# Twelve first units of weights loaded one stage ahead, two loading stages folded away, and sixteen places for the gathers of a mixture of experts

## The reference, cut to what matters

```python
def reference(x, ...):
    x = first_block(x, ...)    # x + [sparse attention | gated MLP] @ w_out, then x + conv feed-forward (width 2816)
    x = second_block(x, ...)   # four mixers, each w_branch product gated by sigmoid(x @ w_gate + b), w_out, layer norm;
                               # then x + sigmoid(x @ w_ple_gate + b) * (p @ w_ple), layer norm
    return third_block(x, ...) # modulated norm of x and of a context of 256 tokens, projections, two attentions, w_out,
                               # then a mixture of experts, and a last rms norm

def moe(h, ...):               # 32 experts, the 4 best of each token
    top_v, top_i = lax.top_k(h @ router_w + router_b, 4)
    ...                        # rows sorted by expert in blocks of 128, each block through its expert
    contrib = ys[dest] * gate_sorted[:, None]
    return jax.ops.segment_sum(contrib, tok_sorted, num_segments=T)
```

## Time and profile before

| | |
|---|---|
| median of 3 runs | 4125.99 us (4120.43 to 4131.15) |
| the profiled execution | 4129.73 us, its span 4127.9 us |
| PE busy | 3511.0 us (85%) |
| DVE busy | 2328.0 us (56%) |
| ACT busy | 1536.9 us (37%) |
| POOL busy | 140.4 us (3%) |
| mean granted clock of PE | 0.913 of 2.4 GHz |
| DMA | 653.53 MB, 158 GB/s over the span |
| experts' stage | from about 2820 us to 4061 us |

### The profile page before, as it was taken

How to read it: one execution, slowest core, us unless ns; L and a number is a source line. 1 busy time by engine, 2 the same in 40 slices (tenths; PEclk the granted TensorE clock), 3 DMA queues, 4 the chain that set the end, 5 groups by cost and what they waited for, 6 DMA issues and landing times. The chain is left out here.

```text
span 4127.9 us, 45959 instructions
## 1 busy us (share of the span) xinstructions
PE 3511.0 (85%) x15671; PEld 2637.0 (64%) x15672; DVE 2328.0 (56%) x2916; ACT 1536.9 (37%) x1926; POOL 140.4 (3%) x124
## 2 busy tenths in 40 slices
PE   6778798999958688899879778775999999999996
PEld 4646687774446457688652645554777777777774
DVE  3355675338232245445440547435888888888885
ACT  1143332010023431110110215314777777777772
POOL 0000000000000100000000000002000000000001
PEclk8889999999979899699989889977999999999997
DMA  4311222222111100022216300116999999999995
GB/s 144 104 47 42 82 91 93 77 95 82 62 36 46 32 11 1 27 95 99 81 61 232 102 31 19 34 58 273 387 361 366 353 362 365 355 350 363 363 351 197
DMA packets 172315, 653.53 MB, mean 158 GB/s; under 512 B 14953, under 2 KB 82377, under 8 KB 114226
## 3 DMA queue, kind: packets, MB, share of 16 engines
q1 hardware_dynamic: 154370, 605.44, 40.2%
q0 software_dynamic: 7568, 25.70, 1.7%
q10 hardware_dynamic: 10272, 20.98, 1.3%
HBM read 610.98 MB, written 36.77 MB: 157 GB/s over the span
## 5 line engine op out<-in xcount | busy, mean ns | idle before, releaser
L378 DVE TENSOR_TENSOR experts_rest<-experts_weights,experts_leading 128x2048 fp32r<-128x2048 f32 x384 | 875.3, 2286 | 100.1 <-ACT experts_leading L2894 100.1
L2894 ACT CAST experts_leading<-experts_weights 128x2048 fp32r<-128x2048 f32 x384 | 715.4, 1904 | 46.9 <-ACT experts_y L2886 23.1
L384 PE MATMUL psum<-experts_leading,experts_xT_leading 128*128 128x512 f32 x1024 | 409.3, 400 | 51.6 <-DVE experts_rest L378 51.6
L385 PE MATMUL psum<-experts_rest,experts_xT_leading 128*128 128x512 f32 x1024 | 406.8, 397 | 0.0
L386 PE MATMUL psum<-experts_leading,experts_xT_rest 128*128 128x512 f32 x1024 | 402.5, 393 | 0.0
L384 PEld LDWEIGHTS psum<-experts_leading,experts_xT_leading 128*128 128x128 f32 x1024 | 194.6, 190 | 107.8 <-DVE experts_rest L378 65.4
L386 PEld LDWEIGHTS psum<-experts_leading,experts_xT_rest 128*128 128x128 f32 x1024 | 194.4, 190 | 44.6
L385 PEld LDWEIGHTS psum<-experts_rest,experts_xT_leading 128*128 128x128 f32 x1024 | 194.9, 190 | 40.2
L384 PE MATMUL psum<-experts_leading,experts_hidden_leading 128*128 128x512 f32 x512 | 210.3, 411 | 0.0
L386 PE MATMUL psum<-experts_leading,experts_hidden_rest 128*128 128x512 f32 x512 | 202.0, 394 | 0.0
L385 PE MATMUL psum<-experts_rest,experts_hidden_leading 128*128 128x512 f32 x512 | 200.9, 392 | 0.0
(11 more groups left out here) (664 smaller groups left out, 6923.2 us busy)
## 6 DMA issues: line engine op xcount, KB each, us to landing
experts_weights<-in_w_up SPq DMA_DIRECT2D x256, 1024.0 KB, 6.9
experts_weights<-in_w_down SPq DMA_DIRECT2D x128, 1024.0 KB, 6.8
merge_weights<-in_w_merge SPq DMA_DIRECT2D x32, 768.0 KB, 4.2
ada_weights<-in_w_ada SPq DMA_DIRECT2D x24, 1024.0 KB, 6.8
ff_up_weights<-in_w_up SPq DMA_DIRECT2D x22, 1024.0 KB, 4.8
expert_rows<-experts_y ACTq DMA_DIRECT2D x66, 256.0 KB, 7.2
down_weights<-in_w_down SPq DMA_DIRECT2D x16, 704.0 KB, 5.1
out_weights<-in_w_out SPq DMA_DIRECT2D x6, 1536.0 KB, 8.7
```

The source lines that it names most:

```text
L378: return dve.tensor_tensor(out, src, leading.bitcast(F32), ALU.subtract)
L384: pe.matmul(out, lh, rh, start=start, stop=False)
L385: pe.matmul(out, lh, rl, start=False, stop=False)
L2894: act.copy(leading[h % LEADING], place(ring, h)).then_inc(masked, 1)
```

## The change

`FirstUnit` sets a place for one unit of weights at the top of SBUF (`Core.high`), with semaphores of its own (242 to 247), and `load` issues its DMAs in whatever stage calls it. The stage that uses the unit takes that place as place 0 of its ring and skips the load of unit 0. By the code there are twelve such units: proj1, out1, the up stage, proj2a, proj2b, proj2c, merge, out2, ple, proj3, proj3b and out3. Their loads are issued on SP in the stage ahead: in a norm (proj1, ff_up, proj2c, merge, proj3, proj3b), at the start of an attention (out1, out3), in the short `glu` stage (proj2b), or at the end of SP's list in down1 (proj2a), merge (out2) and out2 (ple).

In the opening of these stages DVE now splits the first cut (or unit) first and then all source chunks; PE waits chunk by chunk. In `feed_forward_up`, `gated_products` (first branch) these waits stand inside the loop body and are passed for every unit.

The per-layer input is loaded in out2, and the stage `ple_in` is gone with its barrier; the context is loaded in the layer norm at the end of the second block (`ln2`), and `ctx_in` is gone; the zeros are cleared by POOL in `rope_diff`. In `combine` there are sixteen places, no gather waits for a sum, and the residual's load waits for the seventh gather.

```diff
+EARLY = (242, 244, 246)
...
+    def high(self, name, shape, below=0):
+        at = self.nc.sbuf_top // 32 * 32 - below - 4 * math.prod(shape[1:])
+        assert self.nc.sbuf_base <= at, name
+        t = self.nc.alloc_sbuf_tensor_at(name, shape, F32, offset=at)
...
         with nc.Block() as block:
-            if memory:
+            if memory or then:
                 @block.sync
                 def _(sp):
+                    if then:
+                        then(sp, sem)
...
+class FirstUnit:
+    def __init__(self, k, name, pieces, size, below=0):
+        self.slot = k.high(f"{name}_first", [P, size], below)
+        self.at = k.places[-1]
+        first = EARLY[k.early % len(EARLY)]
+        k.early += 1
+        self.pieces = pieces(self.slot)
+        self.landed = [k.nc.alloc_semaphore(f"{name}_first{c}_landed", num=first + c) for c in range(len(self.pieces))]
+
+    def load(self, sp, sem):
+        for (place, src), landed in zip(self.pieces, self.landed):
+            sp.dma_start(place, src).then_inc(landed, 16)
+
+    def retire(self, k):
+        k.retired += self.landed
+        k.places.remove(self.at)
+
+def first_unit(k, name, section, below=0, size=None):
+    unit = section.weights[0, :, :]
+    return FirstUnit(k, name, lambda slot: [(section.cut(slot, c), section.cut(unit, c)) for c in range(len(section.cuts))],
+                     size or section.kc * section.columns, below)
...
-def project(k, name, sections, beside=None, room={}):
+def project(k, name, sections, beside=None, room={}, first=None, then=None):
...
-        ring = sb("weights", [P, 2, size])
-        landed = [[sem(f"weights{i}_half{c}_landed") for c in range(2)] for i in range(2)]
+        ring = [first.slot if first and i == 0 else sb(f"weights{i}", [P, size]) for i in range(2)]
+        landed = [first.landed if first and i == 0 else [sem(f"weights{i}_half{c}_landed") for c in range(2)] for i in range(2)]
...
+                        if first and q == 0 and isinstance(u, int) and u == 0:
+                            return
                         sp.wait_ge(emptied[slot], turn * s.chunks + done0[q][slot])
...
-                                half = s.kc // 2 or s.kc
-                                if j == 0 and s.split and source_chunks and kk in (0, half):
-                                    pe.wait_ge(source_split, source_chunks - s.kc + (s.kc if kk else half))
+                                opens = isinstance(u, int) and u == 0
+                                if j == 0 and s.split and source_chunks and (kk == 0 or opens):
+                                    pe.wait_ge(source_split, source_chunks - s.kc + (kk + 1 if opens else s.kc))
...
+                if first:
+                    split_unit(0, 0, starts[0] % 2, 0, only=0)
                 split_source(range(own // 2))
-                split_unit(0, 0, starts[0] % 2, 0, only=0)
+                if not first:
+                    split_unit(0, 0, starts[0] % 2, 0, only=0)
                 split_source(range(own // 2, own))
...
 def feed_forward_up(k, src, out, first):
...
-                            if j == 0 and kk in (0, KD // 2):
-                                pe.wait_ge(source_split, KD if kk else KD // 2)
+                            if j == 0:
+                                pe.wait_ge(source_split, kk + 1)
...
+                split_unit(0, 0)
                 for kk in range(KD):
-                    if kk == KD // 2:
-                        split_unit(0, 0)
                     dve.wait_ge(source_masked, kk + 1)
...
 def gated_products(..., first, then=None):
...
-                            if q == 0 and (j, kk) in ((0, 0), (0, kc_gate // 2), (1, 0)):
-                                pe.wait_ge(source_split, (kc_gate // 2 if kk == 0 else kc_gate) if j == 0 else kc_gate + kc)
+                            if q == 0 and (j == 0 or kk == 0):
+                                pe.wait_ge(source_split, kk + 1 if j == 0 else kc_gate + kc)
...
-                split_source(source_gate, gate_parts, kc_gate // 2, 0)
                 split_unit(0, 0)
-                split_source(source_gate, gate_parts, kc_gate, 0, lo=kc_gate // 2)
+                split_source(source_gate, gate_parts, kc_gate, 0)
                 split_source(source(0), parts[0], kc, kc_gate)
...
-    with k.stage("ple_in", within=True) as (sb, sem):
-        per_layer = sb("p", [P, PLE // P, T])
...
+    def ple_loads(sp, sem):
         landed = sem("p_landed")
+        sp.dma_start(per_layer[:, :, :], k.dram["pT"].rearrange("(c p) t -> p c t", p=P)).then_inc(landed, 16)
+        w_ple.load(sp, sem)
+        sp.wait_ge(landed, 16)
...
+    def ctx_load(sp, sem):
+        landed = sem("ctx_landed")
+        sp.dma_start(cx[:, :, :], k.dram["ctxT"].rearrange("(k p) t -> p k t", p=P)).then_inc(landed, 16)
+        sp.wait_ge(landed, 16)
...
                 sp.dma_start(b2[:, :], k.dram["b2_3"]).then_inc(landed, 16)
+                sp.wait_ge(gathered[N // 2 - 2], 16)
                 sp.dma_start(k.x[:, :, :].rearrange("p k t -> p (k t)"), residual).then_inc(back, 16)
...
-                    if n >= 4:
-                        pool.wait_ge(weighed, n - 3)
-                    pool.indirect_dma_start(out=got[:, n % 4, :], out_offset=None, in_=results,
+                    pool.indirect_dma_start(out=got[:, n, :], out_offset=None, in_=results,
                                             in_offset=bass.IndirectOffsetOnAxis(ap=dest[:, t, c:c + 1], axis=0)
-                                            ).then_inc(gathered[n % 4], 16)
+                                            ).then_inc(gathered[n], 16)
```

## The result

The kernel after takes 4088.03 us (median of 5 runs, 4081.84 to 4098.61), the kernel before 4128.65 in the same comparison (4120.43 to 4131.15). The ratio is 0.9908, 95% interval 0.9888 to 0.9929. The forecast was 4073 with a range of 4062 to 4090. The direction holds and the time lies inside the range, but the forecast itself is 15 us too low. The profiled execution of after took 4088.03 us, 41.7 less than the 4129.73 of before; the sum said 53. (The other 3.7 us are the distance of before's profile from its median, which after's profile does not have.)

A forecast was written before the change was run, and what follows sets the result against it. TensorE was taken to bound the long stages, with gains only at seams: 15.1 + 19.2 + 11.7 + 7 = 53 us off 4129.73, giving 4076.7; less 3.7 us to the median, 4073 us, range 4062 to 4090.

The forecast's parts named there:

- six DVE-led openings: Proj1, out1, proj2a, out2, proj3, out3: without DVE's waits the second block starts 11.9 us after ACT; gain 15.1 us.
- six openings led by PE's start: Up stage, proj2c, ple, proj3b, proj2b and merge: earlier loads and weights split first gain 19.2 us.
- stages that went: Removing the per-layer input stage (4.9 us), its barrier (1.0) and the context stage (5.75) gains 11.7 us.
- gathers: At the end, sixteen gathers issued back to back let the last addition start 7 us earlier, bounds 4 and 10.
- Behind that, DVE splits a unit in 7 us while PE has 16 us of work, so the gain is passed on: Six DVE-led openings: DVE stays ahead of PE after the opening, so the 15.1 us gain is kept.
- named as a rival: The clock falls in new gaps of six openings and merge, about 2 us each, 14 us, 4087; chance 0.2.
- The change does not touch such bodies: Long stages where TensorE is the bound, and the experts' stage: taken as unchanged, only the seams gain.
- PE's waits: Up stage, ple, merge: 228 added waits taken as 0; rival 0.30 us each, 68 us, 4141, chance 0.05.
- The traffic: Gathers: 8.4 MB of rows and 2.1 MB of residual at 408 GB/s need 26 us from 4064.6, ending at 4090.4.
- the residual's wait: Gathers: the residual waits for the seventh gather on SP; nothing queues behind it, and DVE needs it after all sixteen.
- POOL's pace: Gathers: each issue takes 0.94 + 0.30 us, so the last of sixteen is issued near 4082.
- The rule of the Trainium skill: Gathers: DVE's two-port instructions hold up POOL; twelve issues at 1.94 + 0.30 us would shrink 7 to about 1 us.

The follow-up runs named there:

- The experiment with the second column: The kernel after, with VectorE splitting the second column block ahead of the rest in six four-column openings: 4069.42 us, ratio 0.9858 to before.
- The residual first: The kernel after, with the wait ahead of the residual's load taken out, so it is queued with the first gathers: 4083.51 us, one run.
- the residual last: The kernel after, with the residual's load waiting for the sixteenth gather instead of the seventh: 4084.15 us, one run.
- Multiples of 128: The kernel before, with every SBUF tensor placed at a multiple of 128 bytes and nothing else of the change: 4139.25 us, ratio 1.0015.

## Why the prediction was right in direction and wrong in size

The terms of the sum, each read again in the profiled execution of after:

| term | forecast, us | measured, us |
|---|---|---|
| six DVE-led openings, start of the second block | 15.1 | 15.4 |
| clock falls behind it in proj1, out2, proj3 | 0 | -4.9 |
| six openings led by PE's start | 19.2 | 18.2 |
| stages that went | 11.7 | 11.6 |
| gathers | 7 | 3.1 |
| warm pitch of slot 0 | 0 | -6.7 |
| the rest, by subtraction | 0 | 5.0 |
| sum | 53 | 41.7 |

**The openings.** DVE's work was forecast right: 11.91 us from ACT to the second block in all six, where I had 11.9. The single starts were 4.8 in the up stage (forecast 4.9), 3.7 in proj2c (3.8), 3.4 in ple (4.0), 1.7 in proj3b (1.9), 2.7 in proj2b (2.8) and 1.9 in merge (1.8).

**The step that failed first** is "Behind that, DVE splits a unit in 7 us while PE has 16 us of work, so the gain is passed on". It holds for DVE, not for PE's clock. The mechanism was named as a rival, with 1 to 2 us of idle and seven falls at 2 us, 14 us in all. It came in three openings of six, at 1.6 us each. PE starts 3.7 us earlier and the second block only 2.5, so the gap that the change opens is 1.8 to 2.0 us, just where falls begin in these openings. The seventh place that the rival counted, merge, had a gap of 1.98 us and no fall. The experiment with the second column takes the gap away and the falls with it.

**The step that failed most** was put at nothing without a reason. "The change does not touch such bodies" fixed the long stretches behind the openings, and the place of the operands in them was not priced at all; it took 6.7 us. The prediction said of PE's waits that they cost nothing, which is right, and feared a pitch above 0.23 only from them. It read the places in the diff (`high`) as a question of room. The new start of slot 0 is 224 modulo 256, where the other operands of weights are at 192 in the up stage, merge and ple and at 64 in proj1: 3.4 us in merge from its second unit on (253.12 to 256.52 us), 1.3 in the up stage, 0.9 in ple, 1.1 in proj1 (its warm pitches times 192 matmuls in each half of the stage). In out3 and proj3 it changed nothing, since there slot 0 started at 224 before too. For merge this is the whole story: its opening gained what was forecast, and yet the stage lost 1.5 us on balance (from ACT's first copy to the last matmul 267.27 us before, 268.80 after). The experts' matmuls, which the prediction took as fixed, went from 1213.2 to 1214.5 us, first to last.

**The gathers** are a mis-sized term: 3.1 for 7, below the lower bound of 4. Two parts of the working failed. The traffic was taken as 408 GB/s from 1.6 us after the first issue on, an average from slices in which four gathers and the residual were under way; now the residual is not there at the start, and the first eight full slices average 282. That is 1.0 MB short, about 2.5 us at 408 GB/s. And the residual's wait was judged by who queues behind it on SP, not by what it takes from the gathers that run then: four fifths of the bytes for 6 us. The residual first gives 2.9 us of the missing 3.9 back. POOL's pace was right: sixteen issues in 19.7 us. The rule of the Trainium skill ("SBUF — State Buffer", section "SBUF: two separate sides") that a two-port instruction of DVE keeps POOL from writing descriptors is borne out only in small, if at all: beside DVE's sums some issues take up to 1.46 us (1.64 with the residual last), none 1.94, and it changes little. Whether DVE is what lengthens them was not tested.

**The stages that went** gave what was forecast, 4.9, 1.0 and 5.75. **The rest**, 5.0 us, is by subtraction; about 1.5 of it is seen in proj2c behind its first matmul, where the slow matmuls at the start were 6 instead of 13 (and the warm pitch 0.2328 instead of 0.2344, with slot 0 at its new start), and 3.4 from the layer norm behind ple to the place of the context stage, where only the context's load on SP is new. Where the clock rises differs from run to run, but that it was this here is argued, not tested.

## What to carry to other kernels

A move of an operand in SBUF is an edit with a price: before it, write down the starts of all operands of a matmul stage modulo 256, and keep them on one remainder; in this kernel that alone is worth 0.7%. A seam that gets shorter at its front and not at its back opens a gap in PE, so shorten the piece of work that ends the gap too, and reckon with a clock fall of 1.6 us where PE, behind a short first block like these, would stand 1.8 us or more. Of transfers that share the traffic, a load with no hurry goes where the traffic is not full, not where the last ones that someone waits for are under way.

## What the hardware showed that I had not expected

- The distance of back-to-back 128x512 matmuls at the high clock is 0.2267 to 0.2273 us where the four operands' starts agree modulo 256 (the experts, 0.2280, and short proj3b aside), and up to 0.2344 where one differs by 32 to 128 bytes. Even a start shared modulo 128 is not enough: 0.2333 in out1 with 0, 0, 0, 128. Multiples of 128 made the kernel before 0.15% slower.
- In the six openings the clock fell behind every PE gap of 1.93 us or more and behind none of up to 1.70 us. Yet it outlived 1.95 to 2.15 us in merge, ten times of ten, and 2.88 us before the matmuls against the constants. So the length of the gap alone does not settle it; what PE did before it differs between these places, and what of it counts is open.
- The gathers alone, at one issue each 1.24 us, moved 282 GB/s in their first eight full slices and 401 to 426 in the next four. With the residual beside them the sum stayed at some 420, but for 6 us the gathers had only a fifth of it.
